# Filling TensorE's waits with multiplications that nobody reads, in a six-stage transformer kernel

## The reference

```python
def reference(...):
    x = first_block(x, c, ctx, c_ctx, ...)       # 2 layers: attention, LayerNorm, conv FFN, LayerNorm
    return second_block(x, positions_2, ...)     # 2 layers, below; RMS norm at the end

def second_block(x, ...):
    for l in range(2):
        proj = rms_norm_2(x, attn_norm[l]) @ w_in[l]
        h_mla, h_diff, h_ch = jnp.split(proj, [IN_MLA, IN_MLA + IN_DIFF], axis=-1)
        o_mla = rms_norm_2(mla_attention(h_mla, ...), mla_out_norm[l])     # 6 heads
        o_diff = diff_attention(h_diff, ...)                               # 6 heads, two maps each
        o_ch = rms_norm_2(chunk_attention(h_ch, ...), chunk_out_norm[l])   # 4 heads
        x = x + jnp.concatenate([o_mla, o_diff, o_ch], axis=-1) @ w_out[l]
        x = x + conv_ffn_2(rms_norm_2(x, ffn_norm[l]), ...)                # 1024 -> 2 x 2816 -> 1024
    return rms_norm_2(x, final_norm)
```

## Time and profile before

| | us |
|---|---|
| median of 3 runs | 1673.38 (1670.33 to 1673.58) |
| the profiled execution, own time | 1676.23 |
| its span, first to last instruction | 1674.9 |
| PE busy | 1588.4 (95%) |
| DVE busy | 1046.4 (62%) |
| ACT busy | 805.6 (48%) |
| mean granted clock of TensorE | 0.978 |

### The profile page before, as it was taken

How to read it: one execution, slowest core, us unless ns; L and a number is a source line. 1 busy time by engine, 2 the same in 40 slices (tenths; PEclk the granted TensorE clock), 3 DMA queues, 4 the chain that set the end, 5 groups by cost and what they waited for, 6 DMA issues and landing times.

```text
span 1674.9 us, 26675 instructions
## 1 busy us (share of the span) xinstructions
PE 1588.4 (95%) x10738; PEld 1375.7 (82%) x10738; DVE 1046.4 (62%) x1936; ACT 805.6 (48%) x1517; POOL 238.7 (14%) x284
## 2 busy tenths in 40 slices
PE   6999999999999999999899997989999999899998
PEld 4778778877777888887899877868999798689986
DVE  3553856465345425787787676666777667567765
ACT  2323873432233323477465544645555556555553
POOL 1110420011101000012011001232111013221110
PEclk8999999999999999999999998999999999899999
DMA  9557022353564224021455543324555443244552
GB/s 374 220 215 271 18 79 101 151 201 151 201 235 189 80 101 151 26 77 51 167 187 201 178 165 126 130 76 151 181 191 183 167 154 120 83 151 177 180 210 76
DMA packets 39417, 257.25 MB, mean 154 GB/s; under 512 B 5504, under 2 KB 6784, under 8 KB 10496
## 3 DMA queue, kind: packets, MB, share of 16 engines
q1 hardware_dynamic: 36416, 249.61, 40.7%
q0 software_dynamic: 1296, 4.72, 0.9%
q10 hardware_dynamic: 1584, 1.23, 0.2%
HBM read 254.49 MB, written 1.05 MB: 153 GB/s over the span
## 4 chain that ended last, share of the span: by engine, by line
PE 81%; DVE 9%; ACT 5%; DMA 3%; issue 2%; POOL 0%; SPq 0%; DVEq 0%; ACTq 0%
PE ps L478 24%; PE ps L479 24%; PE ps L480 24%; PE ps L494 2%; PE ps L625 1%; ACT arena L1650 1%; PE ps L647 1%; PE ps L634 1%; PE ps L520 1%; PE ps L1057 1%; DVE ps L2002 1%; ACT wh L1302 1%; DMA arena<-in_xT 1%; DVE wl L1743 1%; DMA raw<-in_ev_w_in 1%
## 5 line engine op out<-in xcount | busy, mean ns | idle before, releaser
L1743 DVE TENSOR_TENSOR wl<-raw,wh 128x1024 fp32r<-128x1024 f32 (+2 forms) x324 | 378.3, 1209 | 374.7 <-ACT wh L1302 374.1
L1302 ACT CAST wh<-raw 128x1024 fp32r<-128x1024 f32 (+2 forms) x334 | 328.6, 1033 | 519.1 <-PE ps L480 405.8
L478 PE MATMUL ps<-xh,wh 128*128 128x256 f32 (+1 forms) x1582 | 494.8, 313 | 6.5 <-issue 4.6
L480 PE MATMUL ps<-xh,wl 128*128 128x256 f32 (+1 forms) x1582 | 490.0, 310 | 0.0
L479 PE MATMUL ps<-xl,wh 128*128 128x256 f32 (+1 forms) x1582 | 489.9, 310 | 0.0
L478 PEld LDWEIGHTS ps<-xh,wh 128*128 128x128 f32 x1582 | 303.3, 192 | 31.1 <-issue 13.8
L478 PE MATMUL ps<-wh,xh 128*128 128x512 f32 (+3 forms) x812 | 301.7, 372 | 20.4 <-DVE xl L2134 7.0
L479 PEld LDWEIGHTS ps<-xl,wh 128*128 128x128 f32 x1582 | 303.5, 192 | 15.1 <-issue 0.7
L480 PEld LDWEIGHTS ps<-xh,wl 128*128 128x128 f32 x1582 | 303.4, 192 | 15.2
L480 PE MATMUL ps<-wh,xl 128*128 128x512 f32 (+3 forms) x812 | 296.8, 365 | 0.0
L479 PE MATMUL ps<-wl,xh 128*128 128x512 f32 (+3 forms) x812 | 296.7, 365 | 0.0
(11 more groups left out here) (210 smaller groups left out, 1807.9 us busy)
## 6 DMA issues: line engine op xcount, KB each, us to landing
raw<-in_ada SPq DMA_DIRECT2D x48, 1024.0 KB, 7.1
raw<-in_up SPq DMA_DIRECT2D x44, 1024.0 KB, 5.6
raw<-in_fin SPq DMA_DIRECT2D x44, 1024.0 KB, 4.8
raw<-in_down SPq DMA_DIRECT2D x22, 1024.0 KB, 4.8
raw<-in_fout SPq DMA_DIRECT2D x22, 1024.0 KB, 4.9
raw<-in_win SPq DMA_DIRECT2D x12, 1024.0 KB, 5.0
raw<-in_ev_w_in SPq DMA_DIRECT2D x9, 1024.0 KB, 8.0
raw<-in_wout SPq DMA_DIRECT2D x8, 1024.0 KB, 4.7
```

The source lines that it names most:

```text
L478: e.matmul(out, A[0], B[0], start=first, stop=False)
L480: return e.matmul(out, A[1], B[0], start=False, stop=last)
L1302: e.copy(hi_of(j)[:, a:b], raw_of(j)[:, a:b]).then_inc(*S.hi.up((j, half)))
L1743: e.tensor_tensor(lo_of(j)[:, a:b], raw_of(j)[:, a:b], hi_of(j)[:, a:b].bitcast(F), ALU.subtract).then_inc(*S.lo.up((j, half)))
```

## The change

A new helper `keep(b, n)` waits for bank b and then issues n matmuls of the identity matrix with the first 256 columns of the constants `cs`, both plain float32, into that bank. Nothing reads the result; whatever uses the bank next starts a new sum. No signal is raised. The helper is called at 11 places, with 70 matmuls in all: 10 at A, 22 at B, 6 at F, and in each of the two layers of the second stack 2 (C, G), 3 (D, H), 5 (K, I) and 6 (E, J). In `transposes` the wait for the bank also moves ahead of the wait for the probabilities.

```diff
+        def keep(b, n):
+
+            q.wait_ge(*S.cs.at("cs"))
+            wait_bank(b)
+            for _ in range(n):
+                e.matmul(ps[b][:, 0:256], ident, cs[:, 0:256], start=True, stop=True)
+
...
         mixed("od", "od_w_out", 1, (1, 2))
+        keep(0, 10)
         turn_tiles(("f", 1, 0), 1, 0, t2, range(8), [4, 5, 6, 7])
...
             span[:] = [0, 6]
+            keep(0, (22, 6)[l])
             rms_tiles(("a", l), ("x1", 1) if l == 0 else ("f", 0))
...
             def transposes(i):
                 for m in range(1 if i < 6 else 2):
                     b = 2 + (i % 2 if i < 6 else m)
+                    wait_bank(b)
+                    if i == 10 and m == 0:
+                        keep(b, 3)
                     q.wait_ge(*(S.gps if m else S.vec).at((key, "norm", i)))
-                    wait_bank(b)
...
                 elif i in (4, 5):
+                    if i == 4:
+                        keep(7, 2)
                     column(7, i - 4)
...
+            keep(2, 5)
             for t in (1, 0):
                 out("m", t, [2], True, False, 1)
...
                 out("c", t, [6, 7], True, True, 3)
+            keep(0, 6)
             rms_tiles(("b", l), ("a", l))
```

## The result

| | before | after |
|---|---|---|
| median, first 3 and then 6 runs | 1673.38; 1673.47 (1670.33 to 1673.68) | 1664.32 (1663.57 to 1668.52) |
| ratio of the runs, 95% interval | | 0.9957 (0.9943 to 0.997) |
| profiled execution | 1676.23, span 1674.9 | 1663.76, span 1662.5 |
| mean granted clock | 0.978 | 0.993 |
| PE busy | 1588.4 | 1604.8 |

A forecast was written before the change was run, and what follows sets the result against it. TensorE, busy 95% of the span, bounds the kernel, slowed by low-clock stretches behind waits. Savings of 11.8 us, less 0.3 overrun and 1.0 for remaining falls, give 10.5 off 1676.23; 1.4 more for the median gives 1664.3 us, range 1660 to 1671.

The forecast's parts named there:

- B: Stage boundary behind `down1`, a wait of 11.29 us: filling it was to save 1.1 us.
- C and G: Attention waits of 1.4 us, one per layer, with dense filler products behind: 1.4 us saved each, bounds 1.7 and 0.8.
- the overrun of 0.3 us: All filled waits: time by which the new matmuls would outlast them, 0.3 us in all, taken off the saving.
- A, E, F and J: Four of the five stage boundaries: filling their waits was to save 0.25, 0.3, 0.9 and 0.65 us, in that order.
- The mechanism: TensorE's waits: the new matmuls shorten none, but keep the clock high for the work behind; 11.8 us saved before deductions.
- The price: Time of one new 256-column float32 matmul in the waits: taken as 0.50 us, between 0.475 and 0.56.
- The dense places: Behind attention waits in both layers, 1.5 us saved each; ahead of the second layer's output product, 2.8 us.
- The boundaries: Five stage boundaries, where ACT and DVE pace the transposes: 3.2 us saved together at transposes and first products.
- The step from the profiled execution to the median: Whole kernel: the median lay 2.85 us below the profiled execution; half, 1.4 us, was taken off the forecast.
- Rival 1: Stage boundaries: falls stay because transposes come with pauses; 3.2 us not gained, 1667.5 us; chance 0.18.
- Rival 2: All places: identity products do not hold the clock, or the fall moves to an unfilled pause; 1673 us; chance 0.13.
- Rival 3: Filled waits: new matmuls cost more than their waits, if started at the low clock; slower, 1687 us; chance 0.07.

The follow-up runs named there:

- the part runs: Changed kernel with new matmuls only at the stage boundaries: 1666.45 us, ratio 0.9968; only in the attention and its output product: 1670.48 us, ratio 0.9983.

## Why the prediction was right, point by point

The time, 1664.32 against 1664.3, and the sum from the traces, 10.2 against 10.5, are right. That they agree to 0.02 us is luck: the interval of the gain is 5.0 to 9.5 us, and terms made up for each other. C and G together were put 1.5 us too high; the overrun of 0.3 us that did not come, and 0.7 us more than forecast at A, E, F and J, made up for two thirds of it.

- **The mechanism**: shown. The falls went where the waits were filled, in the part runs too, and nothing was gained by making DVE or ACT end a wait earlier.
- **The price**, 0.50 us: too high. It is 0.432, below the lower end of 0.475. Of the 0.95 us of the earlier trace rows the trace has 0.43 from the first record to the second and 0.52 from there to the next kind of matmul, so that row held a change between two kinds, and halving it halved the change as well. The estimate of 0.43 us by the Trainium skill ("FP8 and Floating Point Precision", TensorE Precision Notes) was the better one, and the trace agrees with it. There was no overrun, so 0.3 us too little was forecast; even at 0.50 us the counts outlast only A's wait, by 0.02.
- **The dense places**: D and H (1.5 each) and I (2.8) came out as forecast, I since the trace had both levels of the same work side by side. At D and H the size is right and its reason is not: the twelve small value matmuls do lose at the low clock. In layer 0 they take 1.10 us from the first to the next product with the clock low for the last 0.65, and 0.81 after the change.
- **C and G**, 1.4 us each, were 0.65: the term most mis-sized, below even its lower bound of 0.8. DVE's chain sets the pace there, which the prediction named but took 0.3 us off for. With DVE (and POOL) relieved a fall costs 1.6 us up to D's wait. That DVE alone is the cause is argued from the waits.
- **The boundaries** came to 3.0 us against 3.2, with B's fall left in place: B gave 0.25 of 1.1. That one of the falls stays, for 1.0 us, was right in size. The prediction looked for it behind the pauses between transposes or in the attention's unfilled waits; it came at B, behind the longest unfilled remainder.
- **The step from the profiled execution to the median**: I took half of 2.85 us as falls that the median does not have. The second profile of before, one more draw, speaks for that: I, G and H did not fall, K did, and the stretch behind A was 2.1 us shorter. The other half looks like chance as well. Up to A's wait the same program took from 801.6 to 807.6 us over twelve profiles, with the low clock at different places of the first stack. Of the 12.4 us between the two first spans, 2.3 are of this kind and have nothing to do with the change.
- **Rival 1** (boundaries not held) is refuted for A, E, F and J. At B a fall stayed in three of four profiles, but the rival's reason, the pauses, does not bring it alone: twice the counts had the pause and no fall. The rule of the Trainium skill on transposes ("TensorE: Matmul & The Clock Gate", Part 4), weighed beside this rival, does not hold here. **Rival 2** is refuted: its gain was 3 us at most, and the interval begins at 5.0. **Rival 3** did not come, but its cost does, as soon as counts are doubled.

What stays open: what in an execution decides between a fall and none behind one and the same wait. The long unfilled waits here, from 2.81 to 11.29 us, all had a fall. Among the shorter ones length does not order them: the 1.4 us at C and G had one in six of eight cases, the 2.6 us at K and I in four of eight. What stands around a wait seems to count too; no run tests it.

## What to carry to other kernels

Where TensorE must wait for another engine and dense work of its own follows, useless matmuls in the wait can keep its clock up; the shortest of the filled waits here was 1.4 us. It is worth nearly half of the low time behind the wait if TensorE sets the pace there (1.55 of 3.41 us at D), and a fifth where another engine does (0.65 of 3.41 at C). Measure the price of one and count so that they end ahead of the wait's end: what does not fit is paid nearly in full, and so is any wait that the useless work brings of its own. One profile of such a kernel shows one draw of the falls, so compare stage by stage from more than one profile, and forecast the median from the usual draw.

## What the runs showed of the hardware

- The low clock is not fixed by the program. The same kernel, profiled twice, had it behind different waits of 1.4 to 2.6 us, and 26 runs of before on one chip spread from 1669.7 to 1678.1 us, with a mean clock from 0.985 down to 0.974 in the slowest.
- A plain float32 matmul of 128 x 128 with 256 columns takes 0.432 us from start to start in a run of its own, in two records, and a transpose of 128 columns 0.109 us at the high clock; at the low one it takes 0.214 ((1.92 - 0.42)/7 for the second eight in the earlier trace rows).
- Transposes hold the clock up as well: through 72 in a row, 8.0 us, it stayed at 1.00, and behind shorter rows of them at the ten other places it was never low.
